# State space layer: 128 steps over pairs of tokens in place of 256 over tokens, with matrices on row and column strips

## What is computed

```
u = xn @ w_in                              # 256 x 1024
mag = exp(dt * lr)
ar, ai = mag * cos(dt * li), mag * sin(dt * li)
coef_re = ((ar - 1.0) * lr + ai * li) / den
coef_im = (ai * lr - (ar - 1.0) * li) / den
bbar = coef * b                            # complex, per group 64 x 16
bu = einsum('gph,blgh->blgp', bbar, ug)
x[t] = a * x[t-1] + bu[t]                  # complex, over 256 tokens
y = einsum('ghp,blgp->blgh', c_re, xr) - einsum('ghp,blgp->blgh', c_im, xi)
y = y + d_skip * u
a, g = split(gelu(y) @ w_glu)
out = a * sigmoid(g)
```

## Time and profile before

| | us |
|---|---|
| three runs, median | 2035.34 (2035.09 to 2041.05) |
| profiled execution | 2035.98 |
| its span | 2034.2 |
| TensorE busy in the span | 1853.2 (91%) |
| VectorE | 1288.9 (63%) |
| ScalarE | 863.4 (42%) |
| GpSimd | 190.4 (9%) |
| TensorE's mean granted clock | 0.950 of 2.4 GHz |

### The profile page before, as it was taken

The page is one execution under the profiler, slowest core; times in us unless marked ns, Lnnn a source line. Parts: engine busy times, 40 slices in busy tenths (PEclk is TensorE's granted clock), DMA queues, the critical chain, the costliest instruction groups (busy, mean ns, idle before and its releaser), DMA issues.

```text
span 2034.2 us, 35301 instructions
## 1 busy us (share of the span) xinstructions
PE 1853.2 (91%) x14595; PEld 1723.9 (85%) x14602; DVE 1288.9 (63%) x1649; ACT 863.4 (42%) x974; POOL 190.4 (9%) x157
## 2 busy tenths in 40 slices
PE   7999999999996776699999998999889899889997
PEld 7989999989996765599998977999875675779997
DVE  5447777868775599757777445777653417555444
ACT  4355555565554000145555345666533223034343
POOL 1001000045003155300001001000000000000000
PEclk9999999999998888799999999999889899789999
DMA  6414544444553111244454514355412108214552
GB/s 247 146 37 171 184 178 175 168 165 176 178 184 143 42 44 62 95 169 156 182 184 165 184 45 148 124 180 178 158 42 106 69 33 310 84 63 167 184 186 83
DMA packets 39619, 284.42 MB, mean 140 GB/s; under 512 B 4528, under 2 KB 4528, under 8 KB 5360
## 3 DMA queue, kind: packets, MB, share of 16 engines
q1 hardware_dynamic: 38880, 279.94, 38.2%
q10 hardware_dynamic: 656, 3.28, 0.4%
HBM read 282.15 MB, written 1.05 MB: 139 GB/s over the span
## 4 chain that ended last, share of the span: by engine, by line
PE 69%; DVE 18%; ACT 6%; POOL 3%; issue 3%; DMA 1%; POOLq 0%; DVEq 0%; ACTq 0%; SPq 0%
PE PS L1495 19%; PE PS L1496 19%; PE PS L1497 19%; DVE wlo L784 4%; ACT whi L341 3%; DVE AR L923 2%; DVE AR L1176 1%; PE PS L1586 1%; DVE AR L1177 1%; PE PS L1678 1%; PE PS L1688 1%; POOL AR L2125 1%; DVE AR L1174 1%; ACT AR L433 1%; PE PS L1916 0%
## 5 line engine op out<-in xcount | busy, mean ns | idle before, releaser
L1495 PE MATMUL PS<-XH,whi 128*128 128x256 f32 (+2 forms) x2696 | 788.5, 292 | 43.1 <-DVE wlo L784 25.6
L1496 PE MATMUL PS<-XL,whi 128*128 128x256 f32 (+2 forms) x2696 | 780.2, 289 | 0.0
L1497 PE MATMUL PS<-XH,wlo 128*128 128x256 f32 (+2 forms) x2696 | 779.8, 289 | 0.0
L784 DVE TENSOR_TENSOR wlo<-raw,whi 128x2048 fp32r<-128x2048 f32 x240 | 555.7, 2319 | 234.7 <-ACT whi L341 234.4
L1495 PEld LDWEIGHTS PS<-XH,whi 128*128 128x128 f32 (+1 forms) x2696 | 524.6, 195 | 54.2 <-issue 40.6
L1496 PEld LDWEIGHTS PS<-XL,whi 128*128 128x128 f32 (+1 forms) x2696 | 524.9, 195 | 4.6 <-issue 0.4
L1497 PEld LDWEIGHTS PS<-XH,wlo 128*128 128x128 f32 (+1 forms) x2696 | 524.2, 194 | 4.2
L341 ACT ACTIVATE whi<-raw 128x2048 fp32r<-128x2048 f32 x240 | 455.9, 1902 | 76.0 <-PE PS L1497 53.8
L1495 PE MATMUL PS<-HH,whi 128*128 128x256 f32 x880 | 253.4, 288 | 12.8 <-DVE HL L943 8.5
L1497 PE MATMUL PS<-HH,wlo 128*128 128x256 f32 x880 | 252.6, 287 | 0.0
L1496 PE MATMUL PS<-HL,whi 128*128 128x256 f32 x880 | 252.4, 287 | 0.0
(11 more groups left out here) (305 smaller groups left out, 1960.8 us busy)
## 6 DMA issues: line engine op xcount, KB each, us to landing
raw<-wst SPq DMA_DIRECT2D x264, 1024.0 KB, 4.8
XT<-x_in SPq DMA_DIRECT2D x2, 512.0 KB, 5.8
AR<-sbc ACTq DMA_DIRECT2D x1, 1024.0 KB, 6.7
...
```

The lines of the kernel that those rows point to most:

```text
L784: dve.tensor_tensor(wlo[:, r, :], raw[:, u % RING, :], whi[:, r, :].bitcast(F32), ALU.subtract)\
L1495: pe.matmul(dst, sh, mh, start=first, stop=False, **kw)
L1496: pe.matmul(dst, sh, ml, start=False, stop=False, **kw)
L1497: return pe.matmul(dst, sl, mh, start=False, stop=last, **kw)
```

## The change

A scan step covers two tokens. The state is kept at every odd token only, with the square of the decay; the even token's input goes into the state through a second set of input matrices multiplied by the decay (`XB[1]`), and the even token's output comes from the state before it through output matrices multiplied by the decay (`C2RE`, `C2IM`) and from its own input through a direct product of 32x32 (`K0T`). So there are 8 steps: 2 chunks of 64 pairs by 4 quarters (now 256 channels each). Input matrices take 32 rows, a strip for each quarter of a channel tile, and go to four banks; outputs of a step go round the four column strips. VectorE does the add and the subtract itself. ScalarE copies the turned matrices. On GpSimd the square sums stand ahead of the fills. Work tiles `W5` are two sets, not three. TensorE has a `modulation` unit in every step, and VectorE the low part of the first gated unit ahead of the last outputs. Further, not shown: the angles and sines of one and of two steps (seven small VectorE operations and two of ScalarE in the gating layer), `complex_product` in `discretize`, and on the host the order of the state groups.

```diff
-    return 2 * (s // 8) + s % 2, s // 2 % 4
+    return s % 2, s // 2
...
-        BRE = ar(B0, KT, 2, P)
-        BIM = ar(B0 + 2048, KT, 2, P)
+        BX = [[ar(B0 + 2048 * (1 - ph) + 1024 * ri, KT, P) for ri in range(2)] for ph in range(2)]
+        C2RE, C2IM = ar(4096, 32, 32), ar(5120, 32, 32)
+        C2D = [ar(B0 + 7168 + 512 * i, 32, 16) for i in range(2)]
         SBC = ar(B0 + 2048, 32, 64)
         PHT = ar(4096, 32, 64)
         PHN = ar(2048, 32, 64)
-        XBR, XBI = ar(4096, 32, 32), ar(5120, 32, 32)
-        BT = [ar(B0 + 512 * i, 32, 16) for i in range(4)]
-        W5 = [[AR[:, 2048 * a + 512 * i:2048 * a + 512 * i + 512] for i in range(4)] for a in range(3)]
+        K0T = VEC[:, VC["conv"]:VC["conv"] + 256].rearrange("p (k n) -> p k n", n=32)
+        XB = [[ar(o + 1024 * ri, 32, 32) for ri in range(2)] for o in (B0, 4096)]
+        X1T = ar(0, 32, 32)
+        BT = ar(B0 + 6656, 32, 16)
+        W5 = [[AR[:, 2048 * a + 512 * i:2048 * a + 512 * i + 512] for i in range(4)] for a in range(2)]
...
+            def turned(ph):
+                if ph == 0:
+                    act.wait_ge(S["s5_set"], 1)
+                act.wait_ge(S["s5_turned"], ph + 1)
+                for ri in range(2):
+                    act.activation(BX[ph][ri], PS[:, 2 * ri:2 * ri + 2, :].rearrange("p a (k n) -> p (a k) n", n=P),
+                                   ACT.Copy).then_inc(S["s5_b"], 1)
...
+                    if n == 1:
+                        turned(0)
...
+                    if b == 2:
+                        ahead(t.u)
...
-            def turned():
-                dve.wait_ge(S["s5_turned"], 1)
-                dve.wait_ge(S["s5_clear"], 1)
-                for i, b in enumerate((BRE, BIM)):
-                    for q in range(4):
-                        r = slice(32 * q, 32 * q + 32)
-                        dve.tensor_copy(b[r, :, q % 2, :],
-                                        PS[r, 2 * i:2 * i + 2, :].rearrange("p a (k n) -> p (a k) n", n=P))\
-                            .then_inc(S["s5_b"], 1)
...
+                    if n == 2:
+                        dve.wait_ge(S["s5_c2"], 4)
...
+                    dve.wait_ge(S["bu_mult"], s + 1)
+                    dve.tensor_tensor(wk[0], wk[0], wk[1], ALU.add)
+                    dve.tensor_tensor(wk[2], wk[2], wk[3], ALU.subtract).then_inc(S["v_ready"], 1)
+                    dve.wait_ge(S["v_ready"], s + 1)
...
+                def outputs(b):
+                    dve.wait_ge(S["y5_ready"], 2 * b + 2)
+                    for kk in range(2):
+                        u5 = U5[:, 2 * b + kk, :].rearrange("p (c e) -> p c e", e=2)
+                        y5 = PS[:, 4 + b % 2, kk * T:(kk + 1) * T].rearrange("p (e c) -> p c e", e=2)
+                        ins = dve.scalar_tensor_tensor(u5, u5, vcol("ssm_d", 2 * b + kk), y5, ALU.mult, ALU.add)
                     ins.then_inc(S["y5_sum"], 1)
...
+                for s in range(8):
+                    products(s)
+                    scans(s)
+                    if s >= 2:
+                        (lows if s % 2 else outputs)(s // 2 - 1)
+                split_lo(t.s)
+                t.s += 1
                 outputs(3)
...
+            def turn(ph):
+                if ph == 0:
+                    pe.wait_ge(S["s5_set"], 1)
+                    pe.wait_ge(S["acc_taken"], t.acc)
+                else:
+                    pe.wait_ge(S["s5_b"], 2)
+                    pe.wait_ge(S["s5_xb"], 1)
...
+                for ri, xb in enumerate(XB[ph]):
                     for k in range(KT):
...
+                        mm = pe.matmul(PS[:, 2 * ri + k // 4, (k % 4) * P:(k % 4 + 1) * P],
+                                       xb[:, 4 * k:4 * k + 4, :].rearrange("p q n -> p (q n)"), ident,
+                                       start=True, stop=True)
                 mm.then_inc(S["s5_turned"], 1)
+            def direct():
+                for k in range(KT):
+                    for ri, cm in enumerate((CRE, CIM)):
+                        for q in range(4):
+                            mm = pe.matmul(PS[32 * q:32 * q + 32, 7, 32 * k:32 * k + 32], XB[0][ri][:, 4 * k + q, :],
+                                           cm[:, 4 * k + q, :], start=(ri == 0), stop=(ri == 1), skip_group_check=True)
+                mm.then_inc(S["s5_k0"], 1)
...
+                    if n == 0:
+                        turn(0)
                     if n == 1:
-                        turn()
+                        direct()
+                    if n == 2:
+                        turn(1)
...
+                def inputs(b):
+                    if b:
+                        pe.wait_ge(S["bu_mult"], 2 * b)
+                    for kk in range(2):
+                        k = 2 * b + kk
+                        for ri in range(2):
+                            o = 256 * ri + 128 * kk
+                            for ph in range(2):
+                                for q in range(4):
+                                    rows = slice(32 * q, 32 * q + 32)
+                                    mm = pe.matmul(PS[:, q, o:o + 128], BX[1 - ph][ri][rows, k, :], U5[rows, k, ph:T:2],
+                                                   start=(ph == 0), stop=(ph == 1), skip_group_check=True)
+                    mm.then_inc(S["bu_ready"], 1)
+                def outputs(s):
+                    c, b = step5(s)
+                    wk = W5[s % 2]
+                    bank = PS[:, 4 + b % 2, :]
+                    kw = dict(skip_group_check=True)
+                    if c == 0:
+                        if b >= 2:
+                            pe.wait_ge(S["y5_sum"], b - 1)
+                        pe.matmul(bank, ZB[:, 0:P], ZB[:, :], start=True, stop=False, **kw)
+                        for kk in range(2):
+                            for q in range(4):
+                                r = slice(32 * q, 32 * q + 32)
+                                pe.matmul(bank[r, kk * T:kk * T + P], K0T[r, 2 * b + kk, :], U5[r, 2 * b + kk, 0:T:2],
+                                          start=False, stop=False, **kw)
+                    pe.wait_ge(S["rot_ready"], s + 1)
+                    pe.wait_ge(S["x5_ready"], s + 1)
+                    n = 64 - c
+                    for kk in range(2):
+                        for i, (cm, cn, x5) in enumerate(((CRE, C2RE, 0), (CRE, C2RE, 2), (CIM, C2IM, 1), (CIM, C2IM, 3))):
+                            for own in (True, False):
+                                for q in range(4):
+                                    pos = 4 * kk + q
+                                    o = kk * T + (P + 64 * c if own else 64 * c + 1)
+                                    w = 64 if own else n
+                                    mm = pe.matmul(bank[32 * q:32 * q + 32, o:o + w], (cm if own else cn)[:, 8 * b + pos, :],
+                                                   wk[x5][:, 64 * pos:64 * pos + w], start=False, stop=(i == 3), **kw)
+                    mm.then_inc(S["y5_ready"], 1)
+                pe.wait_ge(S["s5_c2"], 4)
+                inputs(0)
+                pe.wait_ge(S["silu_c"], 1)
+                for s in range(8):
+                    if s % 2 and s < 7:
+                        inputs(s // 2 + 1)
+                    modulation(s, 7)
+                    outputs(s)
                 for mp in range(4):
-                    features(at=T)
+                    features(mp == 0, 2, T)
...
-                for i, (cf, b) in enumerate(((CFR, bre), (CFI, bim), (CFR, bim), (CFI, bre))):
-                    pool.tensor_tensor(BT[i], b16(cf), b, ALU.mult).then_inc(S["s5_bt"], 1)
-                pool.wait_ge(S["s5_bt"], 4)
...
+            def first_inputs():
+                def b32(v):
+                    return v.unsqueeze(2).broadcast_to([P, 32, 32])
                 pool.wait_ge(S["acc_taken"], 8)
+                (x0, x1), (y0, y1) = XB
+                for y, (c0, c1), op in ((y0, (ARE, AIM), ALU.subtract), (y1, (AIM, ARE), ALU.add)):
+                    pool.tensor_tensor(y, b32(c0), x0, ALU.mult)
+                    link(pool.tensor_tensor(X1T, b32(c1), x1, ALU.mult))
+                    ins = pool.tensor_tensor(y, y, X1T, op)
+                    if op == ALU.subtract:
...
+            def shifted_outputs():
+                pool.wait_ge(S["s5_turned"], 2)
                 link(pool.memset(AR[:, 4096:6144], 0.0))
                 for g in range(2):
                     r = slice(64 * g, 64 * g + 64)
                     h = slice(16 * g, 16 * g + 16)
-                    pool.tensor_tensor(XBR[r, :, h], BT[0][r], BT[1][r], ALU.subtract).then_inc(S["s5_xb"], 1)
-                    pool.tensor_tensor(XBI[r, :, h], BT[2][r], BT[3][r], ALU.add).then_inc(S["s5_xb"], 1)
-                pool.wait_ge(S["s5_xb"], 4)
-                pool.memset(AR[:, B0:B0 + 4096], 0.0).then_inc(S["s5_clear"], 1)
+                    pool.tensor_copy(C2RE[r, :, h], C2D[0][r]).then_inc(S["s5_c2"], 1)
```

(15 more changed lines are left out.)

201 lines of the change are left out of this document (91 added, 110 removed).

## The result

The changed kernel takes 1943.0 us (median of four runs, 1943.0 to 1944.4) against 2035.2 before (2033.6 to 2041.1): 0.9544 of the time, 95% interval 0.9524 to 0.9563. The forecast was 1942, with a range of 1928 to 1968.

The account below looks back on a forecast made before the run. VectorE was taken to bound the token steps (busy 141 of 151 us), TensorE to wait in front of them. Front 11.5 plus loop 83.7 less 1 elsewhere is 94.2; 2036.0 less that is 1941.8, forecast 1942 us, range 1928 to 1968.

Parts of the forecast that it names:

- Front, 11.5: State space layer before the token steps: square sums ahead of the fills, first input product 11.5 us earlier, bounds 8 to 14.
- the direct product: TensorE ahead of the token steps: 128 records of 32 columns taken as 3.6 us, bounds 3.5 and 7.4.
- Loop, VectorE, 18.7 a pair: Token steps: VectorE needs 18.7 us for a pair of steps, four pairs, with low part 1.7 and small adds 0.45.
- Loop, TensorE, 18.2 a pair: Token steps: inputs 2.6, outputs 7.0 with 0.8 more, modulation 7.8 make 18.2 us, just under VectorE's 18.7.
- Records this short stop gaining somewhere: Reason given for taking 128 output records on TensorE as 3.9 us, 30 ns each, within bounds 2.4 to 4.8.
- End of the loop: Last rotation at 74.5 us, TensorE free at 81.2, gated unit's start counted as 82.7; the loop gives 83.7 us.
- Elsewhere, 1 with bounds 0 and 3: Feed-forward layer before: GpSimd's some 20 us more of preparation cost 1 us, bounds 0 and 3.
- A stretch with slack: Gating layer: seven added small VectorE operations cost nothing, or 1.5 us with two small sines if the slack is gone.
- the strips don't run together: Rival, token loop: inputs stay 7.0, outputs 4.8 us, TensorE bounds at 24.4 a pair; 1965 us, chance 0.14.
- The lower clock: Rival, token loop: TensorE stays at 1.2 GHz, a pair takes 28.4 us, 37 more in all; 1979 us, chance 0.06.
- The shifted inputs: Rival, front: GpSimd's shifted inputs come late or the square sums don't get ahead; 1955 us, chance 0.10.
- The slowing by changes of strip: Rival, token loop: each record finishes before the next starts, a pair takes 94 us; 2244 us, chance 0.04.

Follow-up runs that it names:

- the first experiment: Changed kernel, but GpSimd makes the second inputs (XB[1]) before the state space layer's square sums, not behind them: 1960.2 us against 1943.0.

## Why the prediction was right, and where it wasn't

The forecast's sum was 94.2 us and the spans differ by 93.0, but two parts were off in opposite directions: front and loop gave 6.6 us more than forecast, and the layers ahead lost 7.7 more. That the total fell within 1.2 us is luck; either error alone would have put it at about 1935 or 1950, still inside the range.

- **Front, 11.5.** From the last residual sum of the layer before (639.60, and 648.31 after) to the sums' matmuls it was 18.9 us and is 5.5: 13.4 less, as forecast, and the first experiment shows the cause. The way from there to the first input product took 31.0 us and not 34.9. The term that was mis-sized is the direct product: 1.30 us for 128 records, 10 ns each, where I took 3.6 and bounded it from below by 3.5. That is 2.3 of the 3.9 us; the rest is spread over handoffs and the fills of the shifted outputs, which came 6.3 us behind the second turn (7.0). A turn took 3.74 (3.5), and VectorE waited for the shifted output matrices till 683.5, the last thing ahead of the loop, as forecast. The front gave 15.3.
- **Loop, VectorE, 18.7 a pair.** It was 17.0 to 17.4. The low part takes 0.68 us and not 1.7: GpSimd's product, which starts 0.16 us later, is the one that waits (1.65 in place of 1.27). The small adds took 0.25 and not 0.45. The scans at 1.2 were right.
- **Loop, TensorE, 18.2 a pair.** Inputs 2.1 (2.6), outputs 2.1 (3.9), modulation 3.4 to 3.6: 13.9 with the 0.7 of the direct product. "Records this short stop gaining somewhere" was the wrong step: at 16 ns a record the four strips' records start within 20 ns of one another, and the next four follow 56 to 80 ns later. The Trainium skill gives about 60 cycles of overhead a matmul in "TensorEngine Tiling (Array Packing)", "Instruction Overhead"; by my estimate from that, 25 ns at 2.4 GHz, 128 records would have been 3.2 us. The rows say 2.1. Had TensorE been where I put it, it would have been nearly the bound; it has over 3 us of room, of which a pause takes some 2. The clock was 0.93.
- **End of the loop.** The last rotation ended at 70.7 us from the first input product (74.5). GpSimd took 3.31 for its last product, beside the low part of the weights, which I had seen beside the adds in front and not here; and the clock made the last outputs 3.28. TensorE was free at 79.1 (81.2), and the start of the gated unit counts as 79.9 (82.7). The loop gave 86.5 (83.7).
- **Elsewhere, 1 with bounds 0 and 3.** This is the step that failed. FFN 2 lost 7.1, gating 2.3. I priced GpSimd's added 20 us of work by one pair of rows (2.69 against 1.78) where its operations were short. What decides is that its larger operations follow one another, so that each of four VectorE instructions in a row meets one; the experiment that spreads them takes the loss away. "A stretch with slack" in gating was wrong too: it is a chain over VectorE and ScalarE, and seven operations cost 1.5.
- **Rivals.** That the strips don't run together is excluded by 16 and 33 ns a record at the full clock, against 47 and 94 in a row; in the experiments it costs 15.6 for outputs alone and 24.7 for inputs alone, where I gave it 23 for both. The two together were not run. The lower clock came for short stretches behind idle time, not for the loop. The shifted inputs took 16.6 us behind the square sums (18 forecast) and were there 3 us ahead of their need, not nearly 5. The slowing by changes of strip would have decided from 125 ns a record on; the records took 10 to 33.
